# First norm of a transformer layer: x loaded first, scale and shift in four column chunks, the first slot's matmuls by k-tile

## The reference

```python
cond = jax.nn.silu(c)
ada = cond @ w_ada[l] + b_ada[l]                 # w_ada: 1024 x 6144
shift1, scale1, gate1, shift2, scale2, gate2 = jnp.split(ada[:, None, :], N_MOD, axis=-1)
h = rms_norm(x) * (1.0 + scale1) + shift1
proj = h @ w_in[l]                               # w_in: 1024 x 2320
q_a, k_a, v_a, q_g, k_g, v_g, g_out, z_lr = jnp.split(proj, SPLIT_POINTS, axis=-1)
...                                              # window attention and gated linear attention
x = x + gate1 * mix
h = rms_norm(x) * (1.0 + scale2) + shift2
x = x + gate2 * (jnp.square(jax.nn.relu(h @ w_mlp_in[l])) @ w_mlp_out[l])
return rms_norm(x) * final_norm_g
```

## Time and profile before

| | us |
|---|---|
| median of 3 runs | 1111.54 |
| lowest and highest | 1108.22 and 1111.82 |
| the profiled execution's own time | 1111.64 |
| its span, first to last instruction | 1109.5 |
| PE busy in the span | 1039.9 (94%) |
| DVE busy | 702.4 (63%) |
| ACT busy | 462.9 (42%) |
| POOL busy | 94.3 (8%) |

### The profile page before, as it was taken

One profiled execution on the slowest core, in us unless ns is written; L12 is line 12 of the kernel. 1 busy time (PEld: TensorE's weight loads), 2 busy tenths in 40 slices (PEclk: granted clock), 3 DMA queues, 4 the chain that ended last, 5 costly groups with the idle time before them and its releaser, 6 DMA issues.

```text
span 1109.5 us, 12725 instructions
## 1 busy us (share of the span) xinstructions
PE 1039.9 (94%) x4963; PEld 832.3 (75%) x4963; DVE 702.4 (63%) x895; ACT 462.9 (42%) x717; POOL 94.3 (8%) x119
## 2 busy tenths in 40 slices
PE   1699999989999999989999999999989999999995
PEld 1578884866666788777888888888878888888884
DVE  6766663677787542698565565545448944477567
ACT  1641001356677511566545444555334243424342
POOL 0002210012223200000000000000122000001100
PEclk9999999999999999999999999999999999999998
DMA  9918751010000442315543354416897423454623
GB/s 351 306 52 295 240 174 38 1 39 1 1 1 1 150 116 76 152 39 172 189 172 131 133 174 147 173 57 246 316 359 273 147 81 114 152 209 157 222 77 152
DMA packets 87618, 163.17 MB, mean 147 GB/s; under 512 B 15267, under 2 KB 36236, under 8 KB 87564
## 3 DMA queue, kind: packets, MB, share of 16 engines
q1 hardware_dynamic: 75740, 119.90, 31.3%
q0 software_dynamic: 11824, 42.51, 10.7%
HBM read 124.63 MB, written 37.76 MB: 146 GB/s over the span
## 4 chain that ended last, share of the span: by engine, by line
PE 78%; DVE 12%; ACT 4%; DMA 2%; issue 2%; SPq 2%; DVEq 0%; ACTq 0%
PE bank L1029 24%; PE bank L1048 24%; PE bank L784 13%; PE bank L654 10%; DMA x_in<-in_x 1%; PE bank L749 1%; DVE small L1336 1%; DVE prob L1330 1%; DVE x L1650 1%; PE bank L815 1%; PE bank L848 1%; DVE h_lo_T L1486 1%; DMA hid_raw<-hidden_forms 1%; ACT gla_out L1842 1%; PE bank L913 1%
## 5 line engine op out<-in xcount | busy, mean ns | idle before, releaser
L1048 PE MATMUL bank<-dn_hi,hid_hi 128*128 128x512 f32 x448 | 175.1, 391 | 3.5 <-DVE dn_lo L1576 3.5
L1048 PE MATMUL bank<-dn_hi,hid_lo 128*128 128x512 f32 x448 | 175.2, 391 | 0.0
L1048 PE MATMUL bank<-dn_lo,hid_hi 128*128 128x512 f32 x448 | 175.0, 391 | 0.0
L1573 DVE TENSOR_TENSOR hid_lo<-hid_raw,hid_hi 128x2048 fp32r<-128x2048 f32 x28 | 64.1, 2290 | 115.3 <-ACT hid_hi L2010 115.3
L2010 ACT ACTIVATE hid_hi<-hid_raw 128x2048 fp32r<-128x2048 f32 x28 | 53.6, 1915 | 169.7 <-PE bank L1048 154.0
L784 PE MATMUL bank<-w_hi,act_hi 128*128 128x512 f32 x256 | 102.3, 400 | 0.9 <-DVE w_lo L1113 0.9
L1029 PE MATMUL bank<-h_hi_T,up_hi 128*128 128x512 f32 x256 | 100.0, 391 | 1.6 <-DVE h_lo_T L1486 1.5
L1048 PEld LDWEIGHTS bank<-dn_hi,hid_hi 128*128 128x128 f32 x448 | 84.5, 189 | 21.6 <-DVE dn_lo L1576 3.9
L1446 DVE TENSOR_TENSOR up_lo<-up_raw,up_hi 128x1024 fp32r<-128x1024 f32 x48 | 58.7, 1223 | 65.4 <-ACT up_hi L1915 65.4
L784 PE MATMUL bank<-w_lo,act_hi 128*128 128x512 f32 x256 | 99.9, 390 | 0.0
L784 PE MATMUL bank<-w_hi,act_lo 128*128 128x512 f32 x256 | 99.8, 390 | 0.0
(11 more groups left out here) (225 smaller groups left out, 1875.3 us busy)
## 6 DMA issues: line engine op xcount, KB each, us to landing
hidden_forms<-hid SPq DMA_DIRECT2D x56, 512.0 KB, 3.3
hid_raw<-hidden_forms SPq DMA_DIRECT2D x56, 512.0 KB, 4.4
ada_w<-in_w_ada POOLq DMA_DIRECT2D x32, 512.0 KB, 6.6
up_raw<-in_w_mlp_in SPq DMA_DIRECT2D x32, 512.0 KB, 5.3
dn_ring<-in_w_mlp_out POOLq DMA_DIRECT2D x24, 512.0 KB, 4.9
raw<-in_w_in SPq DMA_DIRECT2D x36, 256.0 KB, 5.0
ada_w_first<-in_w_ada SPq DMA_DIRECT2D x8, 1024.0 KB, 10.7
dn_t<-in_w_mlp_out POOLq DMA_DIRECT2D x16, 512.0 KB, 7.0
```

Source lines behind the costliest of these rows:

```text
L1048: mm = pe.matmul(b, (hid_hi, hid_lo)[x][n % 2][:, k, t * P:(t + 1) * P], (dn_hi, dn_lo)[y][n % 2][:, k, :], start=(first and i == 0), stop ...
L1573: v.tensor_tensor(hid_lo[n % 2][:, :, :], hid_raw[n % 2][:, :, :], hid_hi[n % 2][:, :, :], ALU.subtract)\
```

## The change

- SP: the eight tiles of x first (the identity between them), then slot 0's weights, then parts 1 and 0 of w_ada in four chunks of 256 columns each. A chunk is four loads (two halves of k by two parts) with rows of 1 KB. Chunks 2 and 3 lie where x was, so that they wait for the norm of half 0 and of half 1.
- POOL: the first rows of part 2 wait for chunk 3 and for two column sums.
- The norm is done for both halves at once, before w_ada. ACT copies each transposed bank to act_full (turned_out), and frees it. Later it applies scale and shift to a whole k-tile of 1024 tokens in place, then copies to act_hi (norm_hi); DVE subtracts over 1024 tokens (norm_lo).
- The columns of a chunk: DVE multiplies and adds 6 of the 8 row groups on 512 columns, PE adds the other 2 (8 matmuls of 128x1 that read the weights directly) and the sums of DVE's (4 more). A chunk gives scale and shift for two k-tiles.
- Slot 0's matmuls go by k-tile: for each k, half 0 and 1, m 0 and 1, three products, into four banks at once (first_slot). Chunks 2 and 3 stand before k-tile 2 and in the middle of k-tile 4.

```diff
+DVE_K = 6
-    ada_w_first = at(0, "ada_w_first", [2 * KT, D])
+    ada_chunk = [at(o, f"ada_chunk{i}", [KT, HALF]) for i, o in enumerate((130, 146, 64, 80))]
+    chunk_acc = at(202, "chunk_acc", [NCK, HALF])
...
+            def ada_first(c):
+                for j in range(2):
+                    for i, part in enumerate((1, 0)):
+                        cols = part * D + c * 256
+                        sp.dma_start(ada_chunk[c][:, 4 * j:4 * j + 4, i * 256:(i + 1) * 256],
+                                     w_ada_d[:, 4 * j:4 * j + 4, cols:cols + 256]).then_inc(s_ada_first[2 * c + j], 16)
...
+            for t in range(NT):
+                if t == 4:
+                    sp.dma_start(ident[:, :], identity).then_inc(s_ident, 16)
+                sp.dma_start(x_in[:, t, :], x_d[:, t, :]).then_inc(s_x[t], 16)
+            fill(0, 0, columns(w_in_d, QG0))
             ada_first(0)
             sp.dma_start(b_rows, b_ada[0].rearrange("(k p) -> k p", p=P)).then_inc(s_b_rows, 16)
+            ada_first(1)
...
+            sp.wait_ge(s_nrm[0], 1)
+            ada_first(2)
+            sp.wait_ge(s_nrm[1], 1)
+            ada_first(3)
             fill(1, 1, q_columns(0))
...
+            pool.wait_ge(s_ada_first[2 * NCK - 1], 32)
+            pool.wait_ge(s_ada_full, 2)
...
+            def ada_first(c):                                   # PE
+                pe.wait_ge(s_ada_first[2 * c + 1], 32)
+                pe.wait_ge(s_ada_used, DVE_K * c + 1)
+                for k in range(DVE_K, KT):
+                    for i in range(4):
+                        pe.matmul(column(i), ada_chunk[c][:, k, i * P:(i + 1) * P], cond[:, k:k + 1],
+                                  start=(k == DVE_K and i == 0), stop=False, skip_group_check=True)
+                pe.wait_ge(s_ada_used, DVE_K * (c + 1))
+                for i in range(4):
+                    mm = pe.matmul(column(i), chunk_acc[:, c, i * P:(i + 1) * P], ones[:, 0:1], start=False, stop=True,
+                                   skip_group_check=True)
+                mm.then_inc(s_ada_full, 1)
+            def first_slot(k, half):
+                if half == 0:
+                    pe.wait_ge(s_act_lo, k + 1)
+                for m in range(2):
+                    if k == 0:
+                        pe.wait_ge(s_free, G_F + 2 * half + m - 3)
+                    for n, (a, b) in enumerate(((0, 0), (0, 1), (1, 0))):
+                        w = wsl(a, 0)[:, k * 256 + m * P:k * 256 + m * P + P]
+                        mm = pe.matmul(bank[2 * half + m][:, :], w, act(b)[:, k, half * HALF:half * HALF + HALF],
+                                       start=(k == 0 and n == 0), stop=(k == KT - 1 and n == 2), skip_group_check=True)
+                    if k == KT - 1:
+                        mm.then_inc(s_full, 1)
...
+            turn_half(x_nrm, 0, 0, 1)
+            turn_half(x_nrm, 1, KT, 1)
...
+            ada_first(0)
+            ada_first(1)
...
+            pe.wait_ge(s_lo, 1)
+            for k in range(KT):
+                if k == 2:
+                    ada_first(2)
+                first_slot(k, 0)
+                if k == 4:
+                    ada_first(3)
+                first_slot(k, 1)
...
+            for half in range(2):                               # DVE
+                norm_var(half, 0)
+                norm_scale(x_in, x_nrm, half, 0)
+            ada_first(0, range(DVE_K))
             split_lo(0, 0)
             v.wait_ge(s_b_full, 1)
             v.tensor_copy(b_col, bank[5][:, 0:6 * KT]).then_inc(s_b_col, 1)
             v.wait_ge(s_b_col, 1)
+            first_columns(0)
+            ada_first(1, range(DVE_K))
+            norm_lo(0)
+            first_columns(1)
+            norm_lo(1)
+            ada_first(2, range(DVE_K))
+            norm_lo(2)
+            first_columns(2)
+            norm_lo(3)
+            ada_first(3, range(4))
+            norm_lo(4)
+            ada_first(3, range(4, DVE_K))
+            norm_lo(5)
+            first_columns(3)
+            norm_lo(6)
+            norm_lo(7)
...
+            def turned_out(half, k):                            # ACT
+                a.wait_ge(s_full, half * KT + k + 1)
+                a.activation(act_full[:, k, half * HALF:(half + 1) * HALF], bank[(half * KT + k) % 4][:, :], ACT.Copy)\
+                    .then_inc(s_free, 1)
+            def norm_hi(k):
+                a.wait_ge(s_ada_col, 2 * (k // 2 + 1))
+                o = act_full[:, k, :]
+                own.link(a.activation(o, o, ACT.Identity, bias=ada_col[:, k:k + 1], scale=ada_col[:, KT + k:KT + k + 1]))
+                a.activation(act_hi[:, k, :], o, ACT.Copy).then_inc(s_act, 1)
...
+            for half in range(2):
+                for t in range(4 * half, 4 * half + 4):
+                    square(x_in, x_nrm, t, landed_x)
+                norm_root(half, 0)
             for k in range(KT):
+                turned_out(0, k)
+            split_hi(0, 0, None)
             for k in range(KT):
+                turned_out(1, k)
+            a.wait_ge(s_free, 2 * KT)
+            for k in range(KT):
+                norm_hi(k)
             split_hi(1, 1, None)
```

More of the change, by code:

```diff
@@ L719, in turn_half, with column @@
                     mm.then_inc(s_full, 1)
[L721 to L727, removed]
+            def ada_first(c):
+                def column(i):
+                    part = 1 - i // 2
+                    return bank[4][:, part * KT + 2 * c + i % 2:part * KT + 2 * c + i % 2 + 1]
+                pe.wait_ge(s_ada_first[2 * c + 1], 32)
[9 more added lines that the diff above has]
+                mm.then_inc(s_ada_full, 1)
@@ L1130, in ada_part @@
                 acc = ada_acc[:, part % 2, :]
[L1131 to L1135, removed]
-                for k in range(KT):
[L1137 to L1143, removed]
+                if part == 4:
+                    v.wait_ge(s_gate_full, 1)
+                if part == 5:
+                    v.wait_ge(s_ada_full, NCK + 1)
+                for k in range(KT):
+                    j = (part - 2) * KT + k
+                    v.wait_ge(s_ada_w[j % 4], 16 * (j // 4 + 1))
+                    w = ada_w[:, j % 4, :]
                     if k == 0:
@@ L1150, in ada_part @@
                 if part in gate_rows:
[L1151 removed]
+                    v.wait_ge(s_ada_used, ADA_USED + (part - 1) * KT)
                     v.wait_ge(s_ada_b, 16 if part == 2 else 32)
@@ L1178, in norm_scale, with ada_first, first_columns, norm_lo @@
                 ins.then_inc(s_nrm[half], 1)
[L1180 to L1190, removed]
+            def ada_first(c, ks):
+                acc = chunk_acc[:, c, :]
+                for k in ks:
+                    v.wait_ge(s_ada_first[2 * c + k // 4], 32)
+                    w = ada_chunk[c][:, k, :]
+                    if k == 0:
+                        ins = v.tensor_scalar(acc, w, cond[:, k:k + 1], None, ALU.mult)
+                    else:
+                        v.wait_ge(s_ada_used, DVE_K * c + k)
+                        ins = v.scalar_tensor_tensor(acc, w, cond[:, k:k + 1], acc, ALU.mult, ALU.add)
+                    ins.then_inc(s_ada_used, 1)
+            def first_columns(c):
+                v.wait_ge(s_ada_full, c + 1)
+                for part in (1, 0):
+                    cols = slice(part * KT + 2 * c, part * KT + 2 * c + 2)
+                    v.scalar_tensor_tensor(ada_col[:, cols], bank[4][:, cols], float(part), b_col[:, cols],
+                                           ALU.add, ALU.add).then_inc(s_ada_col, 1)
+            def norm_lo(k):
+                v.wait_ge(s_act, k + 1)
+                v.tensor_tensor(act_lo[:, k, :], act_full[:, k, :], act_hi[:, k, :], ALU.subtract).then_inc(s_act_lo, 1)
             v.wait_ge(s_c_exp, 1)
@@ L1220, in features @@
                     v.tensor_copy(dst, bank[2 * half + m][:, :]).then_inc(s_free, 1)
[L1222 to L1226, removed]
             v.wait_ge(s_rows_full, 1)
             v.tensor_copy(rows_sb, bank[7][0:HEADS, 0:384]).then_inc(s_rows, 1)
[L1229 to L1232, removed]
             split_lo(1, 1)
-            features(0, 1, G_F_FIRST[1])
+            for half in range(2):
+                features(0, half, G_F + 2 * half)
             split_lo(2, 0)
```

73 lines of the change are left out of this document (16 added, 57 removed).

## The result

| | before | changed |
|---|---|---|
| median, us | 1111.54 (5 runs, 1108.22 to 1112.57) | 1104.73 (5 runs, 1101.85 to 1105.38) |
| span of the profiled execution | 1109.5 | 1102.9 |
| ratio | | 0.9941, 95% interval 0.9924 to 0.9957 |

Faster, by 6.8 us, where 13.6 were forecast: 1104.73 lies above the range of 1094 to 1104. Two more sets of runs of the same changed kernel, on two chips, had medians of 1100.96 and 1103.32 us, with ratios of 0.9915 (0.9897 to 0.9934) and 0.9928 (0.991 to 0.9946), so the gain is 7 to 9.5 us of some 1111. Both of these medians lie inside the range; that the first lies just outside is in part the draw. The forecast's own figure, 13.6, is missed in all three.

The account below looks back on a forecast made before the run. PE (TensorE, 94% busy) was taken to bound the kernel after the first slot, so only that slot's end counts: 76.2 - 62.6 = 13.6 us less, 1111.6 - 13.6 = 1098.0 us; range 1094 to 1104, about 8 in 10.

Parts of the forecast that it names:

- start of the slot: First slot: after chunk 1's columns, k-tile 0's low part, sums and bias product, PE begins its matmuls at 35.9.
- waits for DVE in it: Inside the first slot: PE reaches k-tile 4 at 49.8, DVE has it ready at 50.1, 0.3 us lost.
- lost to bank 0 behind it: Hand-over to slot 1: bank 0 is free at 62.6 after the slot's end at 62.4, 0.2 us lost.
- the rest of the span: After the first slot: PE mostly sets the rest, so the change only shifts it and all starts 13.6 us earlier.
- 24 products of chunks 2 and 3 at 0.105: Inside the first slot: PE's products and sums for these chunks cost 0.105 us each at the high clock.
- I count that once; bounds are 0 and 3.4: First slot's start: PE's pause brings some 3.2 us at half speed, 1.7 us lost; upper bound means a second fall.
- the interleaved banks cost nothing: First slot: going by k-tile over four banks counted at nothing, since the down projection rotates four banks likewise.
- B: Rival, transposes: clock stays low through all 16 banks, 0.9 us a bank, +3.4 us, 1101.4 us; chance 0.14.
- C: Rival, loads of w_ada chunks: 1 KB rows move at 238 GB/s, +4.8 us, 1102.8 us; chance 0.11.
- D: Rival, loads and first slot: 409 GB/s and no fall of the clock, -0.7 - 1.7 us, 1095.6 us; chance 0.12.
- E: Rival, first slot: clock never rises there, 20.2 us more, slot ends at 82.6, 1118.2 us; chance 0.03.
- F: Rival, after the early start: a later load is late, the 13.6 us gain shrinks to 3 or less; chance 0.03.

Follow-up runs that it names:

- dose kernels: Kernel before, with more one-column products behind slots 2 and 3 (24 and 32 records; second kernel 40 and 24): single profiles, 1112.49 and 1117.19 us.
- fillers: Changed kernel plus matmuls that nothing reads, six behind chunk 0's sums and one behind each product of chunk 1: 1103.86 us, ratio 0.9937.
- all groups on DVE: Changed kernel with all 8 row groups of each chunk on DVE, PE keeping only the 4 sums: 1102.34 us, ratio 0.993.
- spread: Changed kernel with products and sums of chunks 2 and 3 put one by one behind single dense matmuls of k-tiles 1, 3 and 4: 1103.1 us, ratio 0.9934.
- products left out: Changed kernel without PE's 8 products of chunk 2 and of chunk 3, so the output is another: 1096.27 us in one run.
- x late: Changed kernel with the loads of x behind chunk 0: 1107.79 us, ratio 0.9983.
- kernel by halves: Changed kernel with the first slot's matmuls bank by bank again, chunks 2 and 3 in the first bank's run: 1114.48 us, ratio 1.004.
- k-tile 0 ahead: Changed kernel with k-tile 0 ahead of chunk 1's sums and the bias rows' product ahead of chunk 1's: 1101.61 us, ratio 0.9924.
- k-tile 0 ahead with seven groups: Changed kernel, k-tile 0 ahead of chunk 1's sums, DVE's wait for them four row groups later, 7 row groups on DVE: 1097.44 us, ratio 0.988.

## Why the prediction was wrong, point by point

The direction and the chain up to the slot were right; two terms inside the slot were too small, and of one of them, the low clock, the forecast also had only part of the cause.

| step | forecast | measured | difference, us |
|---|---|---|---|
| half 0, half 1 normed | 15.1, 20.7 | 14.6, 19.8 | |
| transposes through | 26.3 | 25.1 | |
| 1 KB rows | 333 GB/s | 347 | |
| multiply-add of 512 columns | 0.75 | 0.751 | |
| affine on 1024 columns | 1.21 | 1.234 | |
| start of the slot | 35.9 | 36.50 | +0.6 |
| 96 matmuls at the high clock | 21.95 | 21.95 to 22.2 (at 9.71/42) | 0 to +0.2 |
| products and sums of chunks 2 and 3 | 2.5 | 5.14 | +2.6 |
| lost by the low clock in the slot | 1.7 | 5.9 | +4.2 |
| waits for DVE in it | 0.3 | 0 | -0.3 |
| end of the slot | 62.4 | 69.55 | +7.1 |
| lost to bank 0 behind it | 0.2 | 0 | -0.2 |
| the rest of the span | 1033.3 | 1033.4 | +0.1 |

- **The step "24 products of chunks 2 and 3 at 0.105".** The rows gave 16 records in 1.68 us, and the change adds 12 instructions a chunk. I divided the time by the records and multiplied by instructions. The kernel before has 8 such products behind a slot and 16 records: the row's own count against the loop's was the check to make. Shown by the chain above and by the dose kernels (24 records, 2.57 us).
- **The step "I count that once; bounds are 0 and 3.4".** Once was three times in two profiles of the changed kernel and twice in the third; 5.9 us were lost, above the upper bound. The forecast tied the fall to PE's pause; the fillers and the dose kernels show that it comes behind records of one column without a pause close ahead. It also took the length from the one fall at 249, 3.2 us (3.4 by the windows there). The stretch ahead of the slot is another case: it lasted 6.8 to 17 us in all, and of the slot 3.1 to 6.0 us of dense matmuls ran at the low level before it ended (the changed kernel 5.0, 5.0 and 3.1; all groups on DVE, spread and fillers 5.3 to 6.0; products left out 3.5), 2.5 us lost in the first profile in place of 1.7.
- **Chunk 1's sums at the low clock** and the bias rows' product (1.87 and 1.37 us at 33.3) stood between DVE and the slot. The forecast had 33.6 to 35.9 there, with the sums at half their records, 0.9 us too little; that DVE was done 0.4 us earlier (33.20) covered part of it. The same count hid another path: PE's own products of chunk 1, 16 records in 3.58 us at the low clock from its landing at 29.64, were through at 33.26, together with DVE. That the order itself was poor, since k-tile 0 needs no chunk 1, neither the forecast nor its rivals said.
- **What the parts are worth.** x first: 4.1 us at the slot's end (69.55 against 73.67). The kernel with x late had one low stretch, this one three; at some 1.65 us for each of the two more, its start alone would be worth 7, which is about the 6.7 by which the start differs, and the 6.8 between the medians on one chip (1107.79 and 1100.96). Executions with the same mean granted clock there, 0.986, differ by as much: 1098.9 to 1099.3 against 1105.6 to 1106.1. The k-tile order over four banks: without it the end is 10 us later and the kernel slower than before. That the interleaved banks cost nothing held nearly: 42 matmuls in 9.69 to 9.71 us are 0.231 each against 0.2286, 0.2 us in the slot.
- **Rivals.** B (clock low through the transposes) did not occur: the transposes of half 1 ran at 2.13/16 = 0.133. C (238 GB/s) did not: 347. Neither half of D (409 GB/s, no fall) did. E had the right place and too high a price for this kernel; in the kernel by halves the clock stayed low for 20.5 us. F did not occur: nothing of the gain at 69.55 was given back.
- **The Trainium skill's rule on transposes** ("TensorE: Matmul & The Clock Gate", Part 4) is contradicted once more, and now without other work on PE ahead: in the profile above that begins with transposes at 14.72, the first 24 take 0.224 us each and the last 16 0.133. That the column reads 1.00 there shows less, since it does so early on at either spacing.

**Still open:** what decides whether 24 records (or 16, or a pause with 8) lower the clock. 24 records in the slot did it at 5 of 6 places in the three profiles of the changed kernel, at 0 of 2 with fillers, at 0 of 2 with x late, at 1 of 2 with k-tile 0 ahead (with a pause of 0.9 us between products and sums); between slots, in the dose kernels, at 0 of 2. No experiment moved the same records in time by small steps.

## What to carry to other kernels

Count a step's records in the trace against the instructions in its loop before pricing one: for the plain float32 products here they are two to one, for the transposes and the split matmuls one to one. Matmuls of one column are dear twice: a record takes 0.105 us where one of 512 columns takes 0.229 (weight loads, PEld, fill the whole time of chunk 2's products and sums, 2.30 us of 44.6 to 46.9), and the clock of the dense work behind them often fell. Letting DVE do more of such a sum helped up to the point where PE waited for it: seven groups with a new order did, eight in the old order did not move the slot's end. And ask of each wait ahead of a long run which of its inputs the first piece needs: putting k-tile 0 ahead of a chunk that only k-tile 2 uses, with the count of products down, brought 5.9 us more in the median than the change had. In the two profiles 3.8 of it lie in the slot (64.20 against 68.00); at the same mean granted clock (0.986 or 0.987) the executions differ by 2.1 to 2.6 us (1097.3 to 1097.7 against 1099.8 and 1099.9), and the rest is less time at the low clock.

## What the runs showed of the hardware

- PE's granted clock fell to 0.50 while PE was busy without a pause: at 124.5, in 40 one-column records that began at 122.51, and at 29.4 behind 24 of them. It came back after 3.4 us of dense matmuls in the middle of the slot. Where products and pauses had gone before, 3.1 to 6.0 us of the slot's dense matmuls ran before it did.
- In the kernel by halves it stayed at 0.50 from 44.9 to 65.4, with PE busy 16.48 of 19 us.
- Transposes alone brought PE from 0.224 to 0.133 us each.
- The same program differs from run to run by 3 us or more (1098.9 to 1105.4 for the changed kernel). Part of it lies in the slot: two profiles of it with spans of 1103.0 and 1101.8 differ by 1.5 us at the slot's end, one low stretch. Part lies far behind the change. From the slot's end to the end of the span, by how long the clock was low in there (the stretch at the very end, which all have, left out):

| low in the rest, us | the rest, us | profiles |
|---|---|---|
| 6.8 | 1030.2 to 1031.0 | all groups on DVE, fillers, products left out, x late, k-tile 0 ahead |
| 10.2 | 1031.7 | k-tile 0 ahead with seven groups |
| 13.7 | 1033.3 to 1034.0 | before, changed (three profiles), spread, by halves |

These low stretches fall in four places, 170 to 200, 235 to 260, 500 to 530 and 790 to 830, in some executions and not in others. A change that saves 2 us in the slot hides in that, as the first reordering did; the slot's end in the profile tells it, and so does comparing executions of the same mean granted clock.
